# Sample attention over a paged cache: all keys before all values, keys turned by VectorE in 32x32 blocks, convolution taps by thirds

## The chip, the cores and the metric

The kernel runs on one core of one Trainium2 chip. The metric is the device time in microseconds (us) of one execution, as a median of repeated runs.

## The reference, cut to what matters

The kernel is one inference step of a two-layer decoder. A prompt (1024 tokens) and eight samples (4 tokens each) go through the same weights. The change touches layer 0, where one input projection feeds a gated convolution of width 3 and an attention with 4 heads; each head has two softmaxes whose difference weighs the values. For the samples, 2048 past keys and values of each lie in pages of 128 tokens, found through a page table:

```python
past_k = cache_k[j, page_table].reshape(nb, -1, DA_HEADS, 2 * DA_DIM)   # 8 samples, 16 pages each
keys = jnp.concatenate([past_k, k_rows], axis=1)      # 2048 past tokens and 4 own
s = jnp.einsum('bqhcd,bkhcd->bhcqk', q, keys) * (DA_DIM ** -0.5)
p = jax.nn.softmax(jnp.where(mask, s, -jnp.inf), axis=-1)
w = p[:, :, 0] - lam * p[:, :, 1]
attn = rmsnorm(jnp.einsum('bhqk,bkhe->bqhe', w, vals), subln_g) * (1.0 - lam_init)
y = ext[:, 0:s] * conv_w[0]                           # convolution: ext = [2 old rows, gate_c * xin]
for j in range(1, 3):
    y = y + ext[:, j:j + s] * conv_w[j]
y_conv = gate_b * y
mixed = jnp.concatenate([y_conv, attn], axis=-1) @ w_out
```

A feed-forward part, a second layer of another kind and its feed-forward part follow.

## The kernel before, in words

Activations lie transposed (features on the 128 partitions, 1056 tokens along the row), in three groups of 352 tokens. A projection is cut into *visits* (one block of 1024x128 weights, 512 KB, loaded by `load_tile`, split into two f16 parts by ScalarE in `split_hi` and VectorE in `split_lo`), and a visit into three *units*, one for each group: 24 f16 matmuls (L372), which `pe_halves` issues in two halves of 12. A unit's PSUM bank is drained by ScalarE or VectorE. In the stretch of this case visits 15 to 23 run, 27 units or 54 halves: for each of three groups of 128 convolution channels the gate `gate_c` (drained by ScalarE), `xin` (VectorE multiplies it into `conv_in`) and `gate_b` (VectorE multiplies it with the convolution's result, L1593). All 27 units use PSUM bank 7 alone.

Every engine's program is written out in order. `woven` takes one piece of the attention, then as many half units as a list of numbers says (`SAMPLE_FILL`), on every engine by the same list, so each engine passes the same places in the same order and waits on semaphores there.

The samples' attention (`pe_samples`, `act_samples`, `dve_samples`) runs in two rounds `r_` of four samples. A round has 32 steps for keys: two pages (a page is 128 tokens x 512 numbers of four bytes, 256 KB) are transposed by TensorE into PSUM (L1943), copied to `kt` by ScalarE (L2012) and VectorE (L2072), and scored one step later by four matmuls, one for each head, each in 32 columns of the array (L1931). Then maxima (L2067), exponentials (L2018) and weights (L1962, L1967), between which eight halves of units stand. Then 32 steps for values: two pages each, straight from the ring (L1982). The ring `ring` has 16 pages; `load_page` puts page f into slot f % 16 when `page_used` says that page f-16 is done with. SP and GpSimd issue these loads in turns of two; SP also issues the weight loads of the stretch. The stretch ends with the output projection (mix_ready, the first L372 over `arena`).

`pool_queries` lays out the samples' queries in `q_blk`; `tap` does one of the three convolution taps over all tokens, for a channel group's first unit of `gate_b`.

Of the kernel before, what the change touches and what calls it, by code (L numbers as in the profile page):

```python
# [18 lines left out]
ALU = mybir.AluOpType  # L19
# [59 lines left out]
def build(nc, x_p, x_s, cache_k, cache_v, state_conv, state_C, state_n, state_m, page_table, norms, w_in0,  # L79
# [3 lines left out]
    with ctx:  # L83
# [1359 lines left out]
        sm_max, sm_neg = small[:, 80:85], small[:, 85:86]  # L1443
        sm_sum, sm_scale = small[:, 86:91], small[:, 91:92]
# [4 lines left out]
        q_blk = arena[:, 19, 0:SEQ].rearrange("p (h b n) -> p h b n", h=HEADS, b=NB)  # L1449
        probs = flat2(20)[:, 0:2 * SEQ + TS]  # L1450
        wt = arena[:, 22, 0:SEQ].rearrange("p (k n) -> p k n", k=NPG)
        wt_own = arena[0:TS, 23, 0:64]
        comb = arena[:, 23, 64:128]
        kt = [arena[:, 24 + i, 0:SEQ].rearrange("p (h n) -> p h n", h=HEADS) for i in range(2)]
# [24 lines left out]
        kp_ev = [sem("kp_ev0"), sem("kp_ev1")]  # L1479
        kp_used = sem("kp_used")  # L1480
        own_t, max_ready, exps, comb_ready = sem("own_t"), sem("max_ready"), sem("exps"), sem("comb_ready")
        q_ready, o_zero = sem("q_ready"), sem("o_zero")
# [8 lines left out]
        def act_proj0(act, v0, v1_):  # L1491

            later = None
            for n in range(VISITS[v0].units[0], VISITS[v1_].units[-1] + 1):
# [9 lines left out]
                later = n if v >= CXB and m == 2 else None  # L1504
                yield
# [15 lines left out]
        def dve_proj0(dve, chain, v0, v1_):  # L1521
# [11 lines left out]
            def tap(h, k):  # L1533
                w = gains[:, GC + k * HC + h:GC + k * HC + h + 1]
                yp, ys = conv_y[:, 0:SEQ], conv_y[:, SEQ:T].rearrange("p (b t) -> p b t", b=NB)
                xp, xs = conv_p_in[:, k:k + SEQ], conv_s_in[:, :, k:k + NS]
                if k == 0:
                    dve.tensor_scalar(yp, xp, w, None, ALU.mult)
                    chain.link(dve.tensor_scalar(ys, xs, w, None, ALU.mult))
                elif k == 1:  # L1540
                    dve.scalar_tensor_tensor(yp, xp, w, yp, ALU.mult, ALU.add)
                    chain.link(dve.scalar_tensor_tensor(ys, xs, w, ys, ALU.mult, ALU.add))
                else:
                    chain.mark(dve.scalar_tensor_tensor(yp, xp, w, yp, ALU.mult, ALU.add))
                    dve.scalar_tensor_tensor(ys, xs, w, ys, ALU.mult, ALU.add).then_inc(gate_c_used, 1)
            for n in range(VISITS[v0].units[0], VISITS[v1_].units[-1] + 1):
                v, g, x = UNITS[n].visit, UNITS[n].g, ps[:, UNITS[n].bank, :]
                h, m = (v - CXB) // 3 if v >= CXB else v // 3, v % 3
                if v >= CXB and m == 2 and g == 0:
                    if h == 0:  # L1550
                        dve.wait_ge(q_ready, 1)
# [4 lines left out]
                    tap(h, 0)  # L1556
# [27 lines left out]
                if v >= CXB and m == 2:  # L1584
                    if g == 0:
                        tap(h, 1)
                        tap(h, 2)
                        dve.wait_ge(gate_c_used, h + 1)
                        chain.sync()
                        dve.wait_ge(yb_hi, 3 * h)  # L1590
                        dve.wait_ge(mix_ready, 3 * h)
# [222 lines left out]

        def dve_head(dve, chain, h):
# [24 lines left out]
            for i in range(8):  # L1840
# [3 lines left out]
                if i >= 4:  # L1844
# [4 lines left out]
                    yield  # L1849
                if i < 7:  # L1850
                    for hh, ii in next_scores(h, i):
                        dve_mixed(dve, chain, hh, ii)
                yield

        def pool_queries(pool, chain):

            pool.wait_ge(v_ev, 3 * HEADS - 1)
            drained(pool, last_unit(3 * HEADS - 3))
            chain.link(pool.memset(arena[:, 19, 0:SEQ], 0.0))
            for b in range(NB):  # L1860
                for c in range(2):
                    n = 8 * (b % 4) + 4 * c
                    ins = pool.tensor_copy(q_blk[64 * c:64 * c + 64, :, b, n:n + NS],
                                           qT[64 * c:64 * c + 64, :, SEQ + NS * b:SEQ + NS * b + NS])
            ins.then_inc(q_ready, 1)
# [15 lines left out]
        def sp_samples(sp):  # L1881
            f = RING
            for _ in range(3):
                yield
            for _ in range(2):
                for _ in range(32):
                    if f // 2 % 2 == 0 and f < 2 * NB * NPG:
                        load_page(sp, f)
                        load_page(sp, f + 1)
                    f += 2  # L1890
                    yield
                for _ in range(4):
                    yield
                for _ in range(32):
                    if f // 2 % 2 == 0 and f < 2 * NB * NPG:
                        load_page(sp, f)
                        load_page(sp, f + 1)
                    f += 2
                    yield
                for _ in range(3):  # L1900
                    yield

        def sp_proj0(sp, v0, v1_):
            for v in range(v0, v1_ + 1):
                load_tile(sp, v + 4)
                for _ in range(6):
                    yield

        def pe_samples(pe):
# [12 lines left out]
            pe.wait_ge(q_ready, 1)  # L1922
            for r_ in range(2):
                def scores(q):

                    n, b, j = 32 * r_ + q, 4 * r_ + q // 8, q % 8
                    pe.wait_ge(kp_ev[0], n + 1)
                    pe.wait_ge(kp_ev[1], n + 1)
# [1173 lines left out]
```

## Time and profile before

| | |
|---|---|
| median of 3 runs | 2687.76 us (2687.13 to 2693.2) |
| the profiled execution | 2693.54 us, its span 2691.9 us |
| mean granted TensorE clock | 0.992 of full speed |
| TensorE busy | 2623.9 us of the span |
| VectorE, ScalarE, GpSimd busy | 1242.1, 1026.6, 452.3 us |
| moved by DMA | 266.14 MB |

Engines in profile rows: PE is TensorE's matmul, PEld its weight load, DVE VectorE, ACT ScalarE, POOL GpSimd, SP SyncE. L1982 is a line of the kernel. A matmul of four-byte numbers shows as two records. A row of a group of instructions has the count behind an x; times are in us unless said.

### The profile page before, as it was taken

To read this page: it belongs to the slowest core of one execution; us is meant where nothing else is said; L and a number is where in the kernel's file an instruction comes from. 1 tells how busy PE (TensorE), PEld (TensorE's weight loads), DVE (VectorE), ACT (ScalarE), POOL (GpSimd) and SP (SyncE) were. 2 spreads that over 40 slices of the span, in tenths; PEclk is the share of its full clock that TensorE was granted. 3 is DMA by queue.
4 is the path that set the end of the run, shared out by engine and by line. 5 is a ranking of instruction groups with operands and counts; after the bars stand their busy time and mean duration, and the time that the engine had idled before them with its cause. 6 is when DMAs were issued, how large, how long until landed. Compare 5 with 4: busy or idle time off the path is not lost.

```text
span 2691.9 us, 49459 instructions
## 1 busy us (share of the span) xinstructions
PE 2623.9 (97%) x20217; PEld 1876.5 (70%) x20217; DVE 1242.1 (46%) x2042; ACT 1026.6 (38%) x1896; POOL 452.3 (17%) x529
## 2 busy tenths in 40 slices
PE   8999899999999999999999999999999999999998
PEld 5666566656688668886566766667657886788765
DVE  5555532326744214444754434344577441154454
ACT  4455322225444214433443333324365441244333
POOL 4001023222022002311101010110101220123121
PEclk9999999999999999999999999999999999999999
DMA  7211369761211312124434242322411122011442
GB/s 250 63 40 50 98 218 346 242 230 54 75 64 32 81 53 63 48 91 146 122 88 88 40 115 50 96 67 84 151 54 67 64 60 60 32 64 48 134 129 97
DMA packets 257659, 266.14 MB, mean 99 GB/s; under 512 B 10668, under 2 KB 217810, under 8 KB 256796
## 3 DMA queue, kind: packets, MB, share of 16 engines
q1 hardware_dynamic: 231772, 166.10, 22.0%
q0 software_dynamic: 25088, 94.79, 10.0%
q8 instruction: 162, 2.65, 0.4%
q10 hardware_dynamic: 576, 2.10, 0.2%
q14 instruction: 61, 0.50, 0.1%
HBM read 227.45 MB, written 35.50 MB: 98 GB/s over the span
## 4 chain that ended last, share of the span: by engine, by line
PE 90%; DVE 5%; ACT 2%; issue 1%; DMA 0%; POOL 0%; SPq 0%; DVEq 0%; ACTq 0%; POOLq 0%
PE ps L372 49%; PE ps L1130 25%; PE ps L1943 2%; PE ps L1931 1%; PE ps L1629 1%; PE ps L1982 1%; PE ps L1708 1%; PE ps L2477 1%; PE ps L2457 1%; PE ps L2491 1%; PE ps L2513 1%; DVE arena L883 1%; PE ps L1694 1%; PE ps L2500 1%; DVE hT L887 1%
## 5 line engine op out<-in xcount | busy, mean ns | idle before, releaser
L372 PE MATMUL ps<-u,w_split 128*128 128x352 f16 (+1 forms) x4752 | 752.3, 315 | 9.8 <-DVE u L737 5.9
L372 PEld LDWEIGHTS ps<-u,w_split 128*128 128x128 f16 (+1 forms) x4752 | 462.5, 98 | 260.3 <-issue 20.8
L372 PE MATMUL ps<-arena,w_split 128*128 128x352 f16 x3663 | 560.6, 313 | 3.7 <-DVE w_split L345 1.5
L372 PEld LDWEIGHTS ps<-arena,w_split 128*128 128x128 f16 x3663 | 357.6, 98 | 200.8 <-issue 9.5
L1130 PE MATMUL ps<-hT,w_split 128*128 128x264 f16 x3456 | 400.6, 276 | 3.2 <-ACT arena L1170 3.2
L1130 PEld LDWEIGHTS ps<-hT,w_split 128*128 128x128 f16 x3456 | 337.8, 98 | 54.8 <-DVE w_split L345 2.1
L345 DVE SCALAR_TENSOR_TENSOR w_split<-w_raw,w_split 128x1024 f16<-128x1024 f32 (+2 forms) x133 | 184.5, 1388 | 296.4 <-ACT w_split L329 295.8
L1130 PE MATMUL ps<-u,w_split 128*128 128x264 f16 x2592 | 303.4, 276 | 0.0
L1130 PEld LDWEIGHTS ps<-u,w_split 128*128 128x128 f16 x2592 | 253.6, 98 | 38.3
L329 ACT ACTIVATE w_split<-w_raw 128x1024 f16<-128x1024 f32 (+2 forms) x133 | 155.5, 1171 | 135.9 <-PE ps L372 97.3
L343 DVE SCALAR_TENSOR_TENSOR w_split<-arena,w_split 128x512 f16<-128x512 f32 x126 | 85.9, 723 | 103.9 <-ACT w_split L323 103.9
L1260 POOL TENSOR_TENSOR arena<-arena 128x512 f32<-128x512 f32 x18 | 22.8, 1265 | 527.2 <-DVE w_split L343 527.2
L343 DVE SCALAR_TENSOR_TENSOR w_split<-w_raw,w_split 128x512 f16<-128x512 f32 x126 | 80.8, 686 | 62.4 <-ACT w_split L323 62.4
L372 PE MATMUL ps<-arena 128*128 128x352 f16 x657 | 102.6, 316 | 0.0
L2327 ACT ACTIVATE arena<-ps 128x352 f32<-128x352 f32 x66 | 30.5, 464 | 179.7 <-PE ps L372 179.7
L817 POOL TENSOR_TENSOR arena<-arena 128x352 f32<-128x352 f32 x53 | 71.3, 1345 | 160.5 <-ACT arena L805 160.3
L1203 DVE TENSOR_TENSOR arena<-ps,arena 128x528 f32<-128x528 f32 x36 | 25.5, 707 | 153.1 <-ACT arena L1170 153.1
L1300 ACT ACTIVATE arena<-ps 128x352 f32<-128x352 f32 x48 | 22.3, 465 | 191.3 <-PE ps L372 191.3
L372 PEld LDWEIGHTS ps<-arena 128*128 128x128 f16 x657 | 64.5, 99 | 37.0 <-issue 3.1
L1216 DVE TENSOR_TENSOR arena<-arena 128x1056 f16<-128x1056 f32 (+1 forms) x60 | 58.3, 972 | 50.4 <-ACT arena L1153 41.4
L372 PE MATMUL ps<-u,arena 128*128 128x352 f16 x504 | 77.5, 313 | 3.2 <-ACT arena L1298 2.7
L323 ACT ACTIVATE w_split<-arena 128x512 f16<-128x512 f32 x126 | 71.7, 620 | 13.7 <-PE ps L1130 10.9
(405 smaller groups left out, 2989.4 us busy)
## 6 DMA issues: line engine op xcount, KB each, us to landing
w_raw<-in_w_down SPq DMA_DIRECT2D x58, 704.0 KB, 4.7
w_raw<-in_w_in SPq DMA_DIRECT2D x56, 512.0 KB, 7.9
arena<-in_w_gu SPq DMA_DIRECT2D x18, 1024.0 KB, 5.3
w_raw<-in_w_gu SPq DMA_DIRECT2D x18, 1024.0 KB, 5.2
hT<-in_cache_k SPq DMA_DIRECT2D x64, 256.0 KB, 4.4
hT<-in_cache_k POOLq DMA_DIRECT2D x64, 256.0 KB, 4.6
hT<-in_cache_v SPq DMA_DIRECT2D x64, 256.0 KB, 5.0
hT<-in_cache_v POOLq DMA_DIRECT2D x64, 256.0 KB, 5.5
```

The costliest lines, as they stand in the source:

```text
L323: act.activation(split_of(v, 0).rearrange("p (k n) -> p k n", k=kt), raw_of(v), ACT.Copy, scale=WS).then_inc(w_hi, 1)
L329: act.activation(split_of(v, 0)[:, 0:kt * n], raw_of(v), ACT.Copy, scale=WS).then_inc(w_hi, 1)
L343: dve.scalar_tensor_tensor(lo, raw_of(v), WS, hi, ALU.mult, ALU.subtract).then_inc(w_ready, 1)
L345: dve.scalar_tensor_tensor(split_of(v, 1)[:, 0:kt * n], raw_of(v), WS, split_of(v, 0)[:, 0:kt * n], ALU.mult, ALU.subtract).then_inc(w_rea ...
L372: ins = pe.matmul(ps[0:m, bank, 0:GW], split_of(v, wp)[:, k * w + col * P:k * w + col * P + m], x[:, xp, k0 + k, cols(g)], start=(k == 0 a ...
L817: pool.tensor_tensor(sum_y, sum_y, sq_y[k % 2], ALU.add).then_inc(y_added, 1)
L883: ins = dve.scalar_tensor_tensor(h_tmp[:, k % 2, :], ybuf[:, k, cols(g)], gains[:, col:col + 1], rs[0], ALU.mult, ALU.mult)
L887: dve.tensor_tensor(h, h, h_tmp, ALU.add).then_inc(h_ready, 1)
L1130: ins = pe.matmul(ps[:, bank + s_, 0:HW], split_of(v, wp)[:, k * P:(k + 1) * P], x, start=(name in ("M1", "M2", "M5") and k == 0 and q == ...
L1216: dve.tensor_tensor(hi_lo[:, 1], x, hi_lo[:, 0], ALU.subtract).then_inc(hid_ready, 1)
L1943: ins = pe.transpose(ps[:, 4 + e, h * P:(h + 1) * P], ring[:, f % RING, h * P:(h + 1) * P], ident[:, :])
L2327: act.activation((q_of[h % 2], k1, v1, o1)[m // 2][:, m % 2, cols(g)], ps[:, UNITS[n].bank, 0:GW], ACT.Sigmoid if m >= 6 else ACT.Copy, sc ...
```

## The change

All 128 pages of keys of the eight samples come first, then all 128 pages of values. A key page pair is turned by one VectorE instruction (`dve_turn`), which transposes each 32x32 block in place of the whole; so partition group i (32 partitions) holds, 32 features at a time, the tokens of group i, and a score is summed over four matmuls of 32 rows each, against query layouts that are rotated by 32 partitions (`q_turned`, made by DMA). Eight pages are scored together by 64 matmuls, in 4 row groups x 4 column groups, with row group i writing PSUM bank i. Turns run four steps ahead of the scores in VectorE's order. The two softmaxes stand among the key steps and the value steps, at step 32 and step 64. The weight loads of the stretch move from SP to ScalarE, the query copies ahead of the last head's stores on GpSimd, and the taps are done for a third of the tokens ahead of each unit of `gate_b`.

```diff
+        Q_ROWS = (10, 12, 13, 14)
+        q_turned = [arena[:, row, 0:SEQ].rearrange("p (h b n) -> p h b n", h=HEADS, b=NB) for row in Q_ROWS]
+        O_BANK = (6, 3)
+        turned = [rows(19 + 4 * i, 4)[:, :, 0:SEQ] for i in range(2)]
...
@@ act_proj0
+                if v >= CXB + 3 and g == 1:
+                    load_tile(act, v + 4)
@@ dve_proj0
-            def tap(h, k):
+            def tap(h, k, g):
...
+                a, b = g * GW, min(g * GW + GW, SEQ)
+                parts = [(conv_y[:, a:b], conv_p_in[:, k + a:k + b])]
...
-                    tap(h, 0)
+                if v >= CXB and m == 2:
+                    tap(h, 0, g)
...
+                    chain.sync()
+                    tap(h, 1, g)
+                    chain.sync()
+                    tap(h, 2, g)
+                    chain.sync()
...
+        def dve_turn(dve, q):
+            f = 2 * q
+            dve.wait_ge(page_loaded[f % RING // 2], 32 * (f // RING + 1))
+            if q >= 8:
+                dve.wait_ge(scored, q // 4 - 1)
+            dve.transpose(turned[q // 4 % 2][:, q % 4, :],
+                          ring[:, f % RING:f % RING + 2, :].rearrange("p r c -> p (r c)")).then_inc(page_used, 2)
@@ dve_head
+                if h == HEADS - 1 and i == 7:
+                    dve_turn(dve, 0)
@@ pool_queries
-            pool.wait_ge(v_ev, 3 * HEADS - 1)
+            pool.wait_ge(s_done, 16 * (HEADS - 1))
...
+            for s_ in range(1, 4):
+                cut = P - 32 * s_
+                pool.dma_start(arena[0:cut, Q_ROWS[s_], 0:SEQ], arena[32 * s_:P, Q_ROWS[0], 0:SEQ]).then_inc(q_ready, 16)
+                pool.dma_start(arena[cut:P, Q_ROWS[s_], 0:SEQ], arena[0:32 * s_, Q_ROWS[0], 0:SEQ]).then_inc(q_ready, 16)
-        ROUND_FILL = ((0,) * 32 + (2, 2, 2, 2) + (1, 0) * 15 + (0, 0) + (1, 1, 1))
-        SAMPLE_FILL = (1, 1, 0) + ROUND_FILL * 2
+        SAMPLE_FILL = ((1, 1, 0)
+                       + ((0, 0, 0, 1) + (0, 0, 0, 2)) * 3 + (0, 0, 0, 1) + (0, 0, 0, 4)
+                       + ((0, 0, 0, 1) + (0, 0, 0, 2)) * 4
+                       + (0, 0, 2, 0, 0, 0) * 10 + (0, 0, 2, 1)
+                       + (1, 1, 1))
@@ load_page
-            cache, b, p = (cache_k, cache_v)[f // 64 % 2], 4 * (f // 128) + f // NPG % 4, f % NPG
+            cache, b, p = (cache_k, cache_v)[f // (NB * NPG)], f // NPG % NB, f % NPG
@@ pe_samples
+            def scores(n):
+                b, j = n // 2, n % 2
+                pe.wait_ge(page_used, 8 * n + 8)
+                pe.wait_ge(exps, 9 * (n // 8))
+                pages = turned[j].rearrange("p a (e c) -> p a e c", e=2)
+                for s_ in range(4):
                     for h in range(HEADS):
+                        for i in range(4):
+                            part_, e0 = slice(32 * i, 32 * i + 32), P * h + 32 * ((i + s_) % 4)
+                            ins = pe.matmul(ps[32 * h:32 * h + 32, i, 256 * j:256 * j + 256],
+                                            q_turned[s_][part_, h, b, :], pages[part_, :, :, e0:e0 + 32],
+                                            start=(b % 4 == 0 and j == 0 and s_ == 0),
+                                            stop=(b % 4 == 3 and s_ == 3), skip_group_check=True)
+                ins.then_inc(scored, 1)
...
+            for q in range(64):
+                if q % 4 == 3:
+                    scores(q // 4)
+                if q % 32 == 31:
+                    own_scores(q // 32)
+                if q == 35:
+                    first_weights(0)
+                if q == 39:
+                    last_weights(0)
+                yield
+            for q in range(64):
+                values(q)
+                if q == 3:
+                    first_weights(1)
+                if q == 7:
+                    last_weights(1)
+                if q == 39:
+                    out_turned(0)
+                yield
@@ act_samples
+            def exponentials(r_):
                 act.wait_ge(max_ready, r_ + 1)
...
+                for i in range(4):
+                    for a in range(2):
+                        act.activation(probs[a].rearrange("p (f i t) -> p i f t", i=4, t=32)[:, i],
+                                       ps[:, i, 256 * a:256 * a + 256].rearrange("p (f t) -> p f t", t=32), ACT.Exp,
+                                       bias=sm_neg, accum_out=sm_sum[:, 2 * i + a:2 * i + a + 1]).then_inc(exps, 1)
...
+            for q in range(128):
+                if q in (32, 64):
+                    exponentials(q // 32 - 1)
...
@@ dve_samples
+            def maxima(r_):
                 dve.wait_ge(own_t, r_ + 1)
...
+            for q in range(128):
+                if q in (32, 64):
+                    maxima(q // 32 - 1)
+                if q in (33, 65):
+                    scales(q // 32 - 1)
+                if 5 <= q + 4 < 64:
+                    dve_turn(dve, q + 4)
...
@@ sync
-            woven(sp_samples(sp), sp_proj0(sp, CXB + 3, WO0 - 1), SAMPLE_FILL)
+            sp_samples(sp)
```

Turns 1 to 4 stand among the last head's tail in `dve_samples`, and turn 0 in `dve_head`.

## Rows read from the trace of the kernel before

**Rows 1.** The page: busy time, share of the span, instructions; the chain by engine.
```profile
PE 2623.9 (97%) x20217; PEld 1876.5 (70%) x20217; DVE 1242.1 (46%) x2042; ACT 1026.6 (38%) x1896; POOL 452.3 (17%) x529
...
PE 90%; DVE 5%; ACT 2%; issue 1%; DMA 0%; POOL 0%; SPq 0%; DVEq 0%; ACTq 0%; POOLq 0%
```

**Rows 2.** Busy us of PE, PEld, DVE, ACT, POOL by stage; clock, DMA share, GB/s.
```profile
318.00:367.00 49.00, 49.00 (x492) 31.11 (x491) 22.18 (x33) 18.53 (x31) 16.25 (x31) 0.99 0.93 314
368.00:391.00 23.00, 20.94 (x165) 14.72 (x162) 4.57 (x13) 6.70 (x15) 0.54 (x1) 0.93 0.21 71
402.00:437.00 35.00, 35.00 (x557) 21.76 (x558) 6.58 (x11) 4.78 (x8) 12.39 (x24) 1.00 1.04 374
447.00:495.00 48.00, 48.00 (x484) 30.58 (x482) 21.95 (x32) 18.04 (x31) 16.13 (x30) 1.00 0.95 322
```

**Rows 3.** TensorE in order of time, keys and first softmax: start, us, what [idle before].
```profile
315.25 3.67 PE L1943 MATMUL ps<-ident,hT 128*128 128x128 f32 x16 [1.86 <-issue]
...
330.01 0.64 PE L1931 MATMUL ps<-arena 128*32 128x256 f32 x8
330.58 1.09 PE L1943 MATMUL ps<-ident,hT 128*128 128x128 f32 x8
331.60 0.64 PE L1931 MATMUL ps<-arena 128*32 128x256 f32 x8
...
369.29 3.75 PE L372 MATMUL ps<-u,w_split 128*128 128x352 f16 x24
373.69 3.74 PE L372 MATMUL ps<-u,w_split 128*128 128x352 f16 x24 [0.65 <-ACT arena L1513]
378.84 0.30 PE L1960 MATMUL ps<-arena 128*32 128x64 f32 x2 [1.41 <-DVE arena L2086]
...
391.55 0.62 PE L1982 MATMUL ps<-hT,arena 128*4 128x128 f32 x16
```

**Rows 4.** TensorE in order of time, values and the end of the stage.
```profile
394.21 1.06 PE L1982 MATMUL ps<-hT,arena 128*4 128x128 f32 x32
395.20 1.96 PE L372 MATMUL ps<-u,w_split 128*128 128x352 f16 x12
397.10 1.06 PE L1982 MATMUL ps<-hT,arena 128*4 128x128 f32 x32
...
563.86 1.96 PE L372 MATMUL ps<-u,w_split 128*128 128x352 f16 x12
...
574.38 12.59 PE L372 MATMUL ps<-arena,w_split 128*128 128x352 f16 x72 [0.77 <-DVE arena L3016]
```

**Rows 5.** Waits, 300 to 575 us: us in total, times, longest.
```profile
POOL hT L1878 <- PE ps L1943: 134.3, 61, 64.0
```

**Rows 6.** Score matmuls (L1931) and weight loads under way, in slices of 0.03 us.
```profile
330.01:330.04 0.03, 0.03 (x4) 0.03 (x5) 1.00 0.53 205
330.04:330.07 0.03, 0.03 (x4) 0.03 (x8) 1.00 1.06 410
...
330.22:330.25 0.03, 0.03 (x5) 0.00 (x0) 1.00 0.89 342
```

**Rows 7.** TensorE in order of time, last head: row groups, and the tail's wait.
```profile
285.87 1.99 PE L1629 MATMUL ps<-arena 64*128 64x512 f32 x8
287.79 0.28 PE L1632 MATMUL ps<-causal,ident_b 128*128 128x128 bf16 x2
...
310.37 0.66 PE L1643 MATMUL ps<-ident,arena 128*128 128x128 f32 x4 [2.88 <-DVE arena L1806]
```

**Rows 8.** Groups of instructions, 312 to 574 us: busy us, mean ns of one.
```profile
L2067 DVE TENSOR_REDUCE small<-ps 128x1 f32<-128x512 f32 x8 | 5.5, 683 | 0.4 <-PE ps L1931 0.4
L2018 ACT ACTIVATE arena<-ps,small 128x512 f32<-128x512 f32 x8 | 5.4, 685 | 1.6 <-DVE small L2080 1.6
L1541 DVE SCALAR_TENSOR_TENSOR arena<-arena,gains 128x1024 f32<-128x1024 f32 x3 | 3.8, 1279 | 0.0
L1538 DVE TENSOR_SCALAR arena<-arena,gains 128x1024 f32<-128x1024 f32 x3 | 2.2, 748 | 0.0
```

More of the change, by code:

```diff
@@ L1881, in sp_samples @@
         def sp_samples(sp):
[L1882 to L1907, printed above, removed]
+            for f in range(RING, 2 * NB * NPG, 4):
+                load_page(sp, f)
+                load_page(sp, f + 1)
         def pe_samples(pe):
@@ L1921, in pe_samples @@
             pe.wait_ge(at_lo, 2 * HEADS)
[L1922 to L1928, printed above, removed]
-                    pe.wait_ge(exps, 5 * r_)
-                    for h in range(HEADS):
-                        ins = pe.matmul(ps[32 * h:32 * h + 32, j // 2, 256 * (j % 2):256 * (j % 2) + 256],
-                                        q_blk[:, h, b, :], kt[n % 2][:, h, :], start=(b % 4 == 0 and j % 2 == 0),
-                                        stop=(b % 4 == 3), skip_group_check=True)
-                    ins.then_inc(kp_used, 1)
-                if r_:
-                    pe.wait_ge(os_lo, 1)
-                for q in range(32):
-                    for e in range(2):
-                        f = 128 * r_ + 2 * q + e
-                        page_ready(f)
-                        pe.wait_ge(kp_ev[e], 32 * r_ + q)
-                        for h in range(HEADS):
-                            ins = pe.transpose(ps[:, 4 + e, h * P:(h + 1) * P], ring[:, f % RING, h * P:(h + 1) * P],
-                                               ident[:, :])
-                        ins.then_inc(page_used, 1)
-                    if q:
-                        scores(q - 1)
-                    yield
-                scores(31)
@@ L1993, in pe_samples, with values @@
-                yield
-                yield
+            def values(q):
+                r_, b = q // 32, q // 8 % 4
+                pe.wait_ge(wt_act, r_ + 1)
+                pe.wait_ge(wt_dve, 2 * r_ + 2)
+                pe.wait_ge(o_zero, r_ + 1)
+                for e in range(2):
+                    f, p = NB * NPG + 2 * q + e, (2 * q + e) % NPG
+                    page_ready(f)
+                    for h in range(HEADS):
+                        n = 16 * h + NS * b
+                        ins = pe.matmul(ps[32 * h:32 * h + NS, O_BANK[r_], b * P:(b + 1) * P],
+                                        wt_rows[r_][p // 4][:, p % 4, n:n + NS],
+                                        ring[:, f % RING, h * P:(h + 1) * P], start=(p == 0), stop=False,
+                                        skip_group_check=True)
+                    ins.then_inc(page_used, 1)
+                if q % 8 == 7:
+                    for h in range(HEADS):
+                        n = 16 * h + NS * b
+                        ins = pe.matmul(ps[32 * h:32 * h + NS, O_BANK[r_], b * P:(b + 1) * P], wt_own[r_][:, n:n + NS],
+                                        v_own[:, h, :], start=False, stop=True, skip_group_check=True)
+                    ins.then_inc(o_done, 1)
@@ L2849, in _ @@
             for h in range(HEADS):
+                if h == HEADS - 1:
+                    pool_queries(pool, chain)
                 for ev, src, dst, n in ((v_ev, v_nat, v_p, 2), (k_ev, k_nat, k_p, 2)):
```

217 lines of the change are left out of this document (106 added, 111 removed).

## The prediction

> **What bounds the kernel now.** I read the page first, for the engine that sets the end: TensorE is busy 97% of the span and makes 90% of the chain that ended last [rows 1]. So a change counts where it takes work off TensorE, or keeps it from waiting. Then the stretch that the diff rewrites, the samples' attention, from 315 us (first page turned) to 574.4 us (first output-projection matmul): busy times, clock and transfers by stage [rows 2]. TensorE has no idle time in a key round or a value round, VectorE and ScalarE are less than half busy there, and transfers run at 314 to 374 GB/s; in the softmax between keys and values they fall to 71 GB/s, and TensorE waits some. TensorE in order of time prices the key rounds [rows 3]: a set of scores starts at 330.01, the eight transposes of the next two pages at 330.58, the next scores at 331.60, so two key pages cost 1.59 us, of which 1.02 are transposes. 64 such rounds are 102 us. From 369.29, where the keys are scored, to 391.55, where values begin, pass 22.3 us, which hold four units of projection (8 halves of 1.9 us). The value part [rows 4] gives 0.50 us for two value pages, 1.9 us for half a unit, and 10.5 us from the last value to the end of the stage.
>
> In the waits GpSimd, which issues half of the page loads, waits 134 us in total for TensorE's transposes alone [rows 5]: the ring of 16 pages is full, and transfers follow TensorE. So what TensorE saves per page is worth its time only until transfers themselves can't follow; the best rate shown is 374 GB/s, 0.70 us for a page of 256 KB.
>
> **The change, part by part.** *Scores.* Gone: 512 transposes on TensorE, 64 VectorE copies and 64 ScalarE copies. New: 16 groups of 64 matmuls, each 32 rows, 32 columns of weights and 256 streamed columns, in sixteen tiles (four row groups, four column groups). What does a group cost? In the present scores four column tiles run together: four matmuls are in flight within 30 ns, and the second halves of the four join only 0.21 us later [rows 6]. So a set of four costs what one costs, about 0.43 us, and the start of another tile at most some 8 ns. That row groups run together too is seen in the heads [rows 7]: two row groups stream 1024 columns each, and the next line starts 1.92 us later; at the values' rate (0.22 us for 128 columns) one alone takes 1.74 us, and both in turn 3.5. Sixteen tiles at once give 4 x 0.43 plus start and end, 2.1 us for 8 pages. The bounds: below 1.9; above, four tiles at a time, 16 x 0.45 = 7.2 us (a rival). In between, if each record holds the issue for 27 ns (0.22 us for 8 records), 128 x 27 = 3.45 us. I take 2.1, since starts 8 ns apart are shown. Before, the same 8 pages cost 6.4 us.
>
> *Turns.* VectorE gets 64 block transposes of 128x1024 numbers of four bytes. None is in the trace. The nearest rows [rows 8]: 0.75 us for a one-operand multiply of 128x1024, 1.28 for one with two operands; a second pass over the data would make it 2.5. I take 1.2, with 0.75 and 2.5 kept for the range. With 1.1 us of its other work per unit (6.58 us in 35 us, six units [rows 2]) and the taps, VectorE needs 1.45 us per turn of two pages while keys run; transfers need 1.40, or 1.49 with the weights (nine blocks of 512 KB in the stage, 1.4 us each). So in the key stage TensorE (2 x 2.1 + 3 x 1.9 = 9.9 us for two groups) no longer sets the pace; turns and transfers do, 11.9 us.
>
> Only a page prices the turn itself: the Trainium skill, "Vector Engine (DVE) Microarchitecture Reference", section 3.8, says that the transposing front end sustains one element per cycle and lane; no run here shows it yet, and with the 0.96 GHz of "VectorE: DVE Perf Modes" (Specifications) 1024 elements would be 1.07 us, an estimate, by which the sum would be 3 to 4 us better.
>
> *Taps by thirds* are the same elements in nine pieces in place of six: some 0.3 us more VectorE per visit, hidden under VectorE's waits for units; without that cover nine units would pay 0.1 us each. *Weight loads from ScalarE*: each waits for VectorE's split two visits earlier, behind it stand ScalarE's drains of the gate units; that split comes three units before, so I price it at nothing; late, it would hold the single bank 7 and with it the next unit. On SP nothing but pages is left until the last page, so they no longer stand behind a weight load. *Query copies*: four layouts by 6 small DMAs on GpSimd's queue, in front of the stores of the last head. They need the scores of head 2 only, and GpSimd stands idle there. Nothing.
>
> Now the sum, by the clock of the trace of before.
> 1. Start. Turns 1 to 4 (4.8 us) stand among the last head's tail, where TensorE waits for VectorE already (2.88 us [rows 7]). I place half of them on the path: first scores at 317.4, not 315.25.
> 2. First half of the keys. VectorE is through turn 4 at 318.4, 27 more at 1.49 us end at 358.6; scores 2.1 and own scores 1.2 give 362. Ten half units are inside.
> 3. First softmax. TensorE has four halves to do (7.5, and 0.7 us for the drain of bank 7, as 0.65 in [rows 3]), to 370.2. But VectorE's maxima stand *behind* the drains of these same two units, not in front as now: 0.7 drain, 2.7 for four banks, 0.4 for the rest; then eight exponentials of 256 columns, between half and all of 0.69 us each [rows 8], 4.0 us taken. Scores of the next group wait for them: 378.0. That leaves a hole of 7.8 us in TensorE, where 1.41 us [rows 3] stands now.
> 4. Second half of the keys. VectorE has turns in store (the ring filled during the hole), so TensorE sets the pace: 8 x 2.1 + 10 x 1.9 + 4.4 weights + 1.2 own + four drains of 0.7 = 44.2, to 422.2. VectorE needs 28 x 1.2 + 8 = 41.6.
> 5. Values. The ring is full. In the next 15 us the second softmax lets only 24 value pages be loaded, 104 are left at 437.2: 104 x 0.70 + 4 weight blocks x 1.4 = 78.4, to 515.6, and 2.9 for what TensorE does behind the last pages: 518.5. TensorE by itself would be there at 507 (18.4 to the weights, 56 x 0.50, 20 x 1.9). Transfers win.
> 6. End. 10.5 as now and one more half, 12.4: 530.9 in place of 574.4.
>
> 43.5 us less. After 574.4 nothing is touched. The profiled execution took 2693.5 us (its span 2691.9 and 1.6 around it), 5.8 over the median of 2687.76; I take the saving off the median: 2644.
>
> For step 5 the Trainium skill has another rate: "DMA: Bandwidth & Descriptors", section "Where 436 GB/s comes from", puts what one core gets from HBM at about 358 GB/s. By that the 104 pages take 3.4 us longer. The trace goes above it (374 GB/s over 35 us [rows 2]), and the measurement decides.
>
> **The rivals.** *Four tiles at a time* (slower). If tiles of other row groups in the same columns must wait, or weight loads of the same row group do, a group costs 7.2 us. The loss against my sum is 16 x S - 38.4 us (in the first half S is hidden up to 2.7), which eats the gain at S = 5.2; at 7.2 it is 77, so 33 us slower: 2721. For it: no row shows both kinds of tiling at once. Against it: each is shown alone. 0.06. The Trainium skill speaks for it: "TensorE: Matmul & The Clock Gate", Part 3, says that a weight load overlaps matmuls in flight only when its row group differs, and here four loads with the same rows follow each other. By that rule a group would take 16 x 0.57 = 9.1 us and the kernel 2751; the trace does not agree, since in [rows 6] eight loads over all rows are there while matmuls of the first tiles run.
>
> *The turn takes two passes* (slower). At 2.4 us VectorE becomes the bound of the key stage: 27 x 2.4 + 5 to step 2, 30 us late, 31 more in step 4: 2705. It decides from 2.1 us. For it: four-byte numbers; against it: the other four-byte rows. 0.10.
>
> *Issue-bound scores*, S = 3.45: 17 us less gain, 2661. 0.10.
>
> *Transfers keep to 322 GB/s*, the rate of the second key round [rows 2]: 6 us in step 2, 12 in step 5: 2662. For it: most of the stage ran at that rate; against it: there the ring was what held them. 0.08.
>
> *Engines in step*: with bank 7 the only one for units, a unit's drain by VectorE stands behind four turns, 4.8 us. I count that as hidden, since TensorE waits for those turns anyway; if it isn't, seven such places cost 34 us: 2678. 0.10.
>
> **Numbers.** My forecast has 0.56: 2644, by itself from 2630 (transfers as fast as TensorE in step 5, 12 us) to 2658. A difference under 0.3% (8 us) is about what a measurement can't tell from none. Faster: 0.56 + 0.10 + 0.08 + half of engines in step 0.05 = 0.79; same 0.06 (the other half, and a little); slower 0.15 (0.06 + 0.10, less a little for a mild form). The range 2626 to 2682 holds the forecast and the three faster rivals, and leaves out those at 2705 and above.
>
> **What would show it.** A group of 64 scores at 2 us (4 or more: the rivals); the block transpose at 1.2 us; a TensorE hole near 370 us of some 7 us; transfers above 360 GB/s through the values, with TensorE waiting for pages there. Wrong would make me: turns over 2 us, tiles in turn, or drains that hold bank 7 through the key stage.

## The result and the profile after

The median is 2674.2 us (2667.91 to 2679.49, 7 runs) against 2687.93 for the kernel before on the same chip: ratio 0.9946, 95% interval 0.9932 to 0.9959. The interval lies below 1, so the kernel is faster, by 0.5%. The time is inside the range, but the gain is 13.7 us and not the 43.5 that the prediction worked out.

The group of the turns on the profile page of the changed kernel (busy us, mean ns of one):

```profile
L1832 DVE STREAM_TRANSPOSE arena<-hT 128x1024 f32<-128x1024 f32 x64 | 74.6, 1215 | 9.1 <-PE ps L1938 4.5
```

TensorE by stage, in answer to [rows 2] (us, PE busy, granted clock, DMA share, GB/s): first key half, second key half.

```profile
314.00:362.00 48.00, 42.37 (x1155) 1.00 0.98 341
378.00:436.00 58.00, 50.73 (x1194) 0.92 0.79 270
```

TensorE in order of time, in answer to [rows 3, 4]: stops in the first key half, then from the first own scores to the start of the values.

```profile
332.42 2.63 PE L1938 MATMUL ps<-arena 32*32 32x256 f32 x114 [1.14 <-issue]
...
338.44 1.67 PE L372 MATMUL ps<-u,w_split 128*128 128x352 f16 x10 [1.20 <-issue]
...
344.45 0.65 PE L1938 MATMUL ps<-arena 32*32 32x256 f32 x11 [1.76 <-issue]
...
361.78 0.90 PE L1950 MATMUL ps<-arena 128*32 128x32 f32 x32
362.61 3.75 PE L372 MATMUL ps<-u,w_split 128*128 128x352 f16 x24
367.56 3.74 PE L372 MATMUL ps<-u,w_split 128*128 128x352 f16 x24 [1.19 <-DVE arena L1605]
378.62 4.75 PE L1938 MATMUL ps<-arena 32*32 32x256 f32 x128 [7.32 <-ACT small L2035]
...
407.70 2.76 PE L1938 MATMUL ps<-arena 32*32 32x256 f32 x128
410.39 0.32 PE L372 MATMUL ps<-u,w_split 128*128 128x352 f16 x1
414.01 2.66 PE L372 MATMUL ps<-u,w_split 128*128 128x352 f16 x11 [3.30 <-issue]
416.60 3.35 PE L1938 MATMUL ps<-arena 32*32 32x256 f32 x116
420.30 0.65 PE L1938 MATMUL ps<-arena 32*32 32x256 f32 x12 [0.35 <-issue]
...
425.38 3.37 PE L1938 MATMUL ps<-arena 32*32 32x256 f32 x128
...
430.57 1.98 PE L1938 MATMUL ps<-arena 32*32 32x256 f32 x79
434.06 1.36 PE L1938 MATMUL ps<-arena 32*32 32x256 f32 x49 [1.51 <-issue]
...
436.52 3.75 PE L372 MATMUL ps<-u,w_split 128*128 128x352 f16 x24
440.21 1.49 PE L1979 MATMUL ps<-hT,arena 128*4 128x128 f32 x48
441.63 3.75 PE L372 MATMUL ps<-u,w_split 128*128 128x352 f16 x24
445.31 0.62 PE L1979 MATMUL ps<-hT,arena 128*4 128x128 f32 x16
448.31 0.30 PE L1957 MATMUL ps<-small 128*32 128x64 f32 x2 [2.37 <-DVE small L2116]
```

Three things are to be seen. The hole of 7.3 us ahead of 378.62 is there as forecast, and behind that idle time the group runs 4.75 us: the granted clock is 0.50 from 378 to 384 us, the lower of its two levels, 1.2 GHz. A group of scores (next start less own start) takes 2.69 us, not 2.1. And three times in each key half TensorE stops in the middle of a group or unit with no releaser ("issue"). The stop at 434.06 is in the last group of the second half, after 79 of its 128 records.

The start of the value stage in windows of 4 us, TensorE's waits for pages in it (us in total, times, longest), and its end in order of time:

```profile
436.00:440.00 4.00, 4.00 (x53) 1.00 0.00 0
440.00:444.00 4.00, 4.00 (x66) 1.00 0.47 96
444.00:448.00 4.00, 1.94 (x26) 1.00 0.87 318
448.00:452.00 4.00, 3.69 (x26) 0.62 0.33 119
452.00:456.00 4.00, 4.00 (x73) 0.53 0.50 143
```

```profile
PE ps L1979 <- DMA hT<-in_cache_v: 12.4, 10, 3.7
```

```profile
544.83 3.75 PE L372 MATMUL ps<-u,w_split 128*128 128x352 f16 x24
551.17 3.52 PE L372 MATMUL ps<-u,w_split 128*128 128x352 f16 x12 [2.59 <-DVE arena L1605]
...
559.92 0.60 PE L3123 MATMUL ps<-ident,conv_new 128*18 128x128 f32 x4 [2.90 <-DVE arena L1536]
561.30 3.94 PE L372 MATMUL ps<-arena,w_split 128*128 128x352 f16 x14 [0.77 <-DVE arena L3078]
```

In the first 8 us of the value stage almost nothing is transferred. Behind the wait of 2.37 us for the second softmax (at 448.31) the clock is 0.62 and 0.53 from 448 to 456 us, and the transfers are slow again. The stage ends at 561.30, against 574.38 [rows 4] before and 530.9 forecast: 30.4 us later than forecast. Set against the prediction's steps: the second half's first scores 0.6 late (378.62 for 378.0); step 4, from there to the end of the second own scores (436.52), 57.9 for 44.2, 13.7 more; step 5, to the last value (544.83), 108.3 for 96.3, 12.0 more; step 6 16.5 for 12.4, 4.1 more. From the stage's end to the end of the span it is 2113.9 us, 2117.5 before; in the experiments it lies between 2111 and 2118 whatever was edited, and no cause is sought in it. All readings in order of time are of one profiled execution for each kernel (2676.81 us for the changed one).

### The profile page after: what moved, and what is told of

It reads as the page before. It is cut to its first block, busy times and chain, and to the rows that moved or that the text cites. A ratio compares the mean times of both kernels' runs of the same rounds, so it can differ in the third digit from the quotient of the medians.

```text
span 2675.2 us, 51317 instructions
## 1 busy us (share of the span) xinstructions
PE 2572.8 (96%) x21241; PEld 1843.9 (69%) x21241; DVE 1273.7 (48%) x2063; ACT 987.5 (37%) x1848; POOL 454.7 (17%) x535
## 4 chain that ended last, share of the span: by engine, by line
PE 73%; DVE 4%; ACT 2%; issue 1%; POOL 0%; DVEq 0%; ACTq 0%
PE ps L372 40%; PE ps L1130 25%; PE ps L2538 1%; PE ps L2518 1%; PE ps L2552 1%; PE ps L2574 1%; DVE arena L883 1%; PE ps L2561 1%; DVE hT L887 1%; DVE arena L897 1%; PE ps L2602 1%; PE ps L2553 1%; PE ps L786 0%; PE ps L991 0%; DVE w_split L345 0%
## 5 line engine op out<-in xcount | busy, mean ns | idle before, releaser
L1300 ACT ACTIVATE arena<-ps 128x352 f32<-128x352 f32 x48 | 22.2, 463 | 191.4 <-PE ps L372 191.4
L1832 DVE STREAM_TRANSPOSE arena<-hT 128x1024 f32<-128x1024 f32 x64 | 74.6, 1215 | 9.1 <-PE ps L1938 4.5
```

The lines of the kernel that those rows point to most:

```text
L1832: dve.transpose(turned[q // 4 % 2][:, q % 4, :], ring[:, f % RING:f % RING + 2, :].rearrange("p r c -> p (r c)")).then_inc(page_used, 2)
```

## Experiments

The theory after the result: in the second key half TensorE is held by the longer score group and by late instructions, in the value stage by a late start of the transfers and by page waits after which the clock falls. Rivals: the scores' own length explains all of step 4; the transfers' rate explains step 5. All kernels but e2 are edits of the changed kernel.

**e1_maxima_first**: the softmax ahead of the units' drains.

```
 VectorE:  q in (32, 64): maxima -> q in (31, 63);  q in (33, 65): scales -> q in (32, 64)
 ScalarE:  q in (32, 64): exponentials -> q in (31, 63)
```

> The changed kernel with the maxima and exponentials of both softmaxes ahead of the units that follow the last scores of the round, not behind their drains. If the hole of 7.3 us ahead of the ninth score group is made by that order, and TensorE's half clock in the group behind it (4.7 us in place of 2.7) by the hole, both go: the own scores of the second round end 8 to 10 us earlier, at 427 us, and the 2.4 us wait before the second weights too; the kernel is 7 to 11 us faster than the changed one, 2663 to 2667 us. Rival: the turns and the page loads set the pace of the second key half, since VectorE turns nothing during the softmax; then the hole only moves into the key groups behind it, and the gain is under 3 us.

Measured: 2668.54 us, ratio to before 0.9917 (0.9904 to 0.9930). ScalarE, VectorE and TensorE in order of time:

```profile
369.29 1.10 ACT L329 ACTIVATE w_split<-w_raw 128x1024 f16<-128x1024 f32 x1
```

```profile
370.42 1.23 DVE L345 SCALAR_TENSOR_TENSOR w_split<-w_raw,w_split 128x1024 f16<-128x1024 f32 x1 [4.58 <-ACT w_split L329]
```

```profile
373.47 5.50 PE L372 MATMUL ps<-u,w_split 128*128 128x352 f16 x24 [7.76 <-DVE arena L1605]
378.89 2.76 PE L1938 MATMUL ps<-arena 32*32 32x256 f32 x128
```

The hole did not close, it moved: a weight split now stands behind the exponentials on ScalarE, VectorE waits for it with the drain (L1605) behind, and the second unit, which needs the same bank 7, waits for that drain. What was gained lies behind: the wait ahead of the second group's weights (2.37 us at 448.31) is gone, and the values end 100.5 us after the second own scores (433.58) instead of 108.3. Yet the stage opens in the same order and as empty of transfers; what differs comes later, with the clock at 1.00:

```profile
436.00:440.00 4.00, 4.00 (x66) 1.00 0.22 37
...
448.00:452.00 4.00, 4.00 (x43) 1.00 0.92 282
452.00:456.00 4.00, 3.67 (x90) 1.00 1.00 346
```

**e2_taps_only**: the kernel before, with the taps by thirds and nothing else.

```
-def tap(h, k):  whole row, all three thirds at g == 0
+def tap(h, k, g):  one third at each g
```

> The kernel before with nothing but the taps by thirds. In the changed kernel the last head's tail stands 2.8 us earlier than before, ahead of anything of the samples. If that is the taps (three times 1056 elements no longer stand in one piece ahead of the first drain of a gate unit), this kernel is about 3 us faster there and some 0.5 us for each of the three channel groups in the samples' stage: 2683 to 2685 us against 2688. Rival: the 2.8 us come from the query copies and the turn in the head; then it is within 1 us of the kernel before.

Measured: 2688.36 us, ratio 0.9996 (0.9987 to 1.0005). TensorE, the last head and the stage's end:

```profile
307.90 0.66 PE L1649 MATMUL ps<-ident,arena 128*128 128x128 f32 x4 [2.88 <-DVE arena L1812]
...
574.19 6.03 PE L372 MATMUL ps<-arena,w_split 128*128 128x352 f16 x28 [0.77 <-DVE arena L3022]
```

The last head's tail comes 2.5 us earlier than in [rows 7], and the stage ends where it did. The taps alone are worth nothing that can be measured.

**e4_quarter_pages**: only one head of each page (64 KB of 256) is loaded, the rest of the ring keeps old numbers, so scores and values are of wrong data; all instructions stay.

```
-ring[:, f % RING, :], cache[0, ds(page, 1), :, :, :]
+ring[:, f % RING, 0:P], cache[0, ds(page, 1), :, 0:1, :]
```

> The changed kernel with a quarter of each page loaded (the columns of one head; the rest of the ring keeps old numbers, so the outputs of the samples are others). Every instruction of the engines stays. If TensorE's stops in the middle of a score group or of a unit (1.1 to 3.3 us, six of them between 330 and 435 us, with no releaser) are late instruction fetches behind saturated page transfers, they go; if the value stage is held by transfers and by the clock that falls in its waits, it takes TensorE's own 88 to 92 us from the own scores to the last value, not 108. Then the stage ends 25 to 32 us earlier, kernel near 2645. Rival: the stops belong to the stream of small matmuls itself and stay; then only the value stage shrinks and the second key half keeps 58 us.

**e7_half_scores**: leaves out half of the score products (two of four row-group shifts).

```
-for s_ in range(4):
+for s_ in (0, 3):
```

> The changed kernel with two of the four score matmuls of each tile (half of the sum over features is left out, so the outputs of the samples are others). TensorE's instructions in a group fall from 256 with the weight loads to 128. If the scores' own time counts only where TensorE sets the pace, the first key half keeps its length within 2 us (turns and transfers set it), and the second loses 8 times 1.3 us and its stops: own scores of the second round at 420 to 424 us in place of 436.5, kernel 12 us faster than the changed one. Rival: turns set the pace in both halves, then it gains under 4 us.

**e9_half_columns**: all products, each over half of the pages.

```
-ps[32 * h:32 * h + 32, i, 256 * j:256 * j + 256], ... pages[part_, :, :, e0:e0 + 32]
+ps[32 * h:32 * h + 32, i, 256 * j:256 * j + 128], ... pages[part_, 0:2, :, e0:e0 + 32]
```

> Leaves out the scores of half of the pages: each of the 64 products of a score group streams 128 columns instead of 256; the number of instructions is unchanged. If a group is paced by the streamed columns, it takes about 1.4 us like the group with half of the instructions (1.42), and the stops ahead of score groups with no releaser shrink only with the shorter work. If it is paced by the issue of its 128 products and 128 weight loads, it stays at 2.5 to 2.7 us. If the stops come from the fetch of instructions, they remain (some 5 us in the second key half), since just as many instructions are fetched, in less time.

Measured, one run each: e4 2641.62, e7 2652.65, e9 2690.31 us. TensorE's waits with no releaser from 312 to 440 us (us in total, times, longest), in the changed kernel:

```profile
PE ps L1938 <- issue: 7.2, 5, 2.5
PE ps L372 <- issue: 4.5, 2, 3.3
```

in e4, in e7 and in e9:

```profile
PE ps L1938 <- issue: 2.0, 1, 2.0
```

```profile
PE ps L1938 <- issue: 2.5, 1, 2.5
```

```profile
PE ps L1938 <- issue: 16.9, 10, 2.6
PE ps L372 <- issue: 5.3, 2, 4.4
```

The wait of 2 to 2.5 us that all four have is that of the first group, ahead of which the tail ends. The others go when the transfers are a quarter (same instructions) and go when the instructions of the scores are half (full pages); in e7 TensorE waits 8.7 us for turns as well, which leaves instructions time to come. In e9, where the same instructions stand for less work, the waits nearly double: 22.2 us for 11.7. In e9 the second own scores start at 440.29, later than with all columns (435.36), at a clock of 0.84 from 384 to 440. So TensorE here needs instructions faster than they come while pages fill the DMA engines. The instruction queue (q8) fits: in the changed kernel a packet starts in the half microsecond behind 410.9 (queue: packets, MB, share of 16 engines) and takes 1.1 us (13.7% of 16 x 0.5), within the stop that ends at 414.01.

```profile
q8 instruction: 1, 0.02, 13.7%
```

So do the others. Packets of this queue start at 329.76, 336.00, 342.10, 411.38, 417.95 and 431.71 us; each of the six stops ends 1.2 to 1.6 us behind the end of one of these transfers. In e9 all eleven stops behind the first group's do the same (1.2 to 1.5 us).

e4 gives the other shares of step 4: with no stops and a clock of 0.94 the second key half takes 49.1 us, so the longer group and its slow start behind the hole are worth about 5 of the 13.7. A group takes 2.69 us in e4 too, 1.42 with half of the products (and so of the columns), 1.84 with half of the columns alone: fewer columns do not shorten it in proportion, fewer products do. The value stage of e4 takes 88.2 us, with 2.0 us of waits for pages, though the wait for the second softmax (2.4 us) is there.

**e10_heads_inner**: the order of the products.

```
-for h in range(HEADS):
-    for i in range(4):
+for i in range(4):
+    for h in range(HEADS):
```

> The same products in another order: the loop over the four heads (column groups of the array) is inside, the loop over the four row groups outside, so that successive products share their row group. By the rule of the Trainium skill, TensorE: Matmul & The Clock Gate, Part 3, that a weight load is hidden only under a product of another row group, a score group should grow from 2.69 us to 4 or more, the key halves by over 10 us each. If the array takes the sixteen tiles in any order, the group stays at 2.6 to 2.8 us and the time at 2674 within 2.

Measured: 2683.44 us, one run; TensorE in order of time:

```profile
405.46 2.75 PE L1938 MATMUL ps<-arena 32*32 32x256 f32 x128
```

The group is the same, 2.69 us from start to start. The Trainium skill, "TensorE: Matmul & The Clock Gate", Part 3, says that a weight load overlaps products in flight only when its row group differs. By that rule the order should matter; in this kernel's trace it does not. The run is 9 us longer: its stops are elsewhere (12.7 us in all for 11.7; last own scores at 441.03), and the clock is 0.93 in the first key half, where the changed kernel has 1.00. One run does not say more.

**e5_single_halves**: units in the value stage one half at a time.

```
-(0, 0, 2, 0, 0, 0) * 10
+(0, 0, 1) * 20
```

> In the value stage the fill is a half unit after every third pair of pages' step in place of a whole unit after every sixth; the amount of work is the same. If the 16 pages of the ring fill up while TensorE is in a whole unit (3.75 us, 5.6 at the half clock) and it then stands at a page and loses the clock, the time from the end of the second own scores to the end of the values falls from 108 us by 4 to 10, the waits for pages from 12.4 us to under 6, and the median from about 2674 to 2664 to 2670. If the stage is held by the transfers alone, both stay: 108 us and 2674 within 2.

Measured: 2678.05 us, ratio 0.9954 (0.9938 to 0.9971), page waits 13.1 us for 12.4, values 112 us behind the own scores. Missed: whole units between the values are not what holds the stage. What stayed is its start: the first weights still wait, 4.17 us for the softmax, and the clock is 0.84 in the 15 us behind the own scores.

**e11_values_first**: the values open the stage.

```
-(0, 0, 2, 0, 0, 0) * 10 + (0, 0, 2, 1)
+(0,) * 8 + (0, 0, 2, 0, 0) * 11 + (1,)
-TensorE, values: first_weights(1) at q == 3, last_weights(1) at 7
+TensorE, values: first_weights(1) at q == 11, last_weights(1) at 15;  their copies 8 steps later
```

> The value stage begins with eight pairs of value pages in a row; the second group's first weights come after the twelfth pair instead of the fourth, its last weights after the sixteenth instead of the eighth, and the projection units lie behind the first eight pairs, two halves after every third of each five pairs. The work is the same. In the changed kernel the transfers move 0, 96, 318 and 119 GB/s in the four stretches of 4 us from 436, because TensorE opens the stage with a unit and later waits for the second softmax while the ring is full. If that lost start is what step 5 of the prediction left out, the 8 us come back: from the end of the second own scores to the end of the values 98 to 101 us instead of 108, median 2663 to 2667. If the stage is held by the transfers' rate or the clock all through, it stays at 106 to 110 and 2674 within 2.

Measured: 2668.85 us (2661.72 to 2677.12), ratio 0.9924 (0.9894 to 0.9954). Windows, and TensorE in order of time:

```profile
440.00:444.00 4.00, 2.75 (x100) 1.00 0.72 235
...
448.00:452.00 4.00, 4.00 (x42) 1.00 1.03 388
```

```profile
434.24 0.90 PE L1950 MATMUL ps<-arena 128*32 128x32 f32 x32
...
528.55 0.40 PE L1987 MATMUL ps<-arena,small 32*4 32x128 f32 x8
```

From the second own scores to the last value 94 us instead of 108.3 (98 to 101 expected). No weights wait for the softmax; from 450 to 526 us the clock is 1.00 and the transfers run at 368 GB/s, where the changed kernel has 0.88 and 326 GB/s from 451.5 to 540.5. So the transfers can run faster here than in the changed kernel. But the edit opens the transfers earlier and takes away the wait for the softmax, and other kernels part the two: e1 and e12 keep the opening and lose the wait, and take 100.5 and 100.2 us (e8, with half a unit less in front, 99.3). Most of the loss of step 5 is thus the wait and what follows it; what the earlier transfers are worth (here 94 for about 100) is not settled, since e13 below has them too and takes 103. As a time e11 can't be told from the changed kernel: the intervals overlap, and the profiled execution (2664.72) lies below the median.

**e8_unit_earlier**: e1 with one unit moved from the second key half into the first.

```
-((0, 0, 0, 1) + (0, 0, 0, 2)) * 3 + ...        ; ((0, 0, 0, 1) + (0, 0, 0, 2)) * 4
+(0, 0, 0, 2) * 2 + ((0, 0, 0, 1) + (0, 0, 0, 2)) * 2 + (0, 0, 0, 2) + ... ; (...) * 2 + (0, 0, 0, 1) * 4
```

> As e1_maxima_first, with one projection unit moved from the second key half into the first, so that the weight split which stood behind the exponentials on ScalarE in e1 falls into an earlier unit. In e1 the second fill unit waited 7.76 us for a drain that stood behind that split. If this wait is what kept e1 from closing the hole, the second group half of scores starts at about 372.5 instead of 378.9, and the second key half is shorter by one unit (3.9 us): own scores end near 426 against 433.6, median about 2661 to 2664. If the hole is only the softmax's own length (maxima, exponentials, scales), the start stays near 378 and the median within 2 of e1's 2668.5.

Measured: 2670.2 us, ratio 0.9919 (0.9902 to 0.9936). Missed:

```profile
377.75 5.96 PE L372 MATMUL ps<-u,w_split 128*128 128x352 f16 x24 [8.81 <-DVE arena L1605]
```

The split was out of the way, but the same drain stood behind the low part of the unit before (L1536), which waits for ScalarE's high part (L1506), and that stood behind the exponentials.

**e12_hole_closed**: own scores, half a unit, then the softmax; two turns behind the maxima. **e13_both**: with e11. **e14_one_unit**: e13 with one unit in the hole.

```
 all three engines: one more step at q == 31, behind the own scores; there maxima, exponentials; scales at q == 32
 VectorE: turns 34 and 35 behind the maxima
-fill there (0, 0, 0, 4)
+fill there (0, 0, 0, 1, 3)      e14: (0, 0, 0, 1, 1), the other unit at the end of the values
```

> The maxima stand behind the own scores and half a unit, ahead of two of the next turns and of the drain; the exponentials stand right behind the weight split and the high part of that half unit, the scales ahead of the next turns. All units of this stage use one bank, so the second unit in the hole needs the first one's drain: in e1 and e8 that drain stood, by way of the split or the high part, behind the exponentials. If that order makes the hole, the second half's first scores start 9 to 11 us after the first own scores' end instead of 16, at about 372 to 373.5, the half clock there goes, and the median is 2664 to 2668. If the hole is the length of maxima plus exponentials plus scales themselves, the start stays at 378 and the time at e1's 2668.5 or above.

> The edits of e12_hole_closed and e11_values_first together. If the two lie in different stretches, as the stage reading has it, their gains add: 2655 to 2661. If the earlier end of the keys only meets the same transfers sooner, the sum is that of the better one, about 2664 to 2667.

> e13_both with one projection unit in the hole behind the first own scores instead of two; the other unit goes into the value stage, where TensorE stood 14 us at pages in e13. In e12 the second unit of the hole waited 4.19 us for the first one's drain, which stood behind two turns, the weight split and the taps, and then ran 6.3 us at the half clock. If that unit, not the softmax, holds the scores, the second half's scores start 7 to 8 us after the first own scores' end (14.2 in e12, 16.0 in the changed kernel), the keys end 6 to 7 us earlier and, with the unit hidden under page waits, the median is 2657 to 2662. If the value stage has no room for the unit or the clock falls in the shorter hole as well, it stays at e13's 2666 within 2.

Measured: e12 2663.88 us, ratio 0.9897 (0.9881 to 0.9914); e13 2666.44, 0.9904 (0.9887 to 0.9921); e14 2661.55 (2659.25 to 2673.85), 0.9896 (0.9879 to 0.9913). In e12 the scores come 14.2 us behind the own scores (9 to 11 expected, 16.0 in the changed kernel), still behind the second unit. TensorE in e14, and in e13 at the start of the values:

```profile
366.43 3.75 PE L372 MATMUL ps<-u,w_split 128*128 128x352 f16 x24
373.32 4.21 PE L1938 MATMUL ps<-arena 32*32 32x256 f32 x128 [3.14 <-ACT small L2037]
```

```profile
442.73 2.31 PE L1979 MATMUL ps<-hT,arena 128*4 128x128 f32 x32 [3.60 <-DMA hT<-in_cache_v]
446.43 1.03 PE L1979 MATMUL ps<-hT,arena 128*4 128x128 f32 x16 [1.40 <-DMA hT<-in_cache_v]
447.40 5.98 PE L372 MATMUL ps<-u,w_split 128*128 128x352 f16 x24
```

With one unit the scores start 6.9 us behind the own scores (7 to 8 expected), the softmax itself, and the keys end at 428.24 instead of 436.52. But the two gains do not add: in e13 TensorE is through the ring's pages before new ones land, stands 3.60 and 1.40 us, and then runs a unit in 5.98 us where 3.75 is usual (clock 0.50 from 444 to 452); from the own scores to the last value e13 and e14 take 103 us, 9 more than e11 (e14 with one unit more in the stage, and in an execution of 2669.85 us, 8 above its median). e12, e13 and e14 can't be told from each other; the intervals of all three lie below that of the changed kernel.

## Why the prediction was right in direction and wrong in size

**Steps 1 and 2 were right in their sum, by luck.** The first own scores end at 362.61 (362 forecast). But the first scores start at 314.18 and not at 317.4, and the half takes 48.4 us for 44.6. Step 2 had turns and transfers set the pace, "11.9 us" for two groups; in this half TensorE waits for no turn and no page. It set the pace itself, with groups of 2.69 us and three stops for instructions (1.14 + 1.20 + 1.76 = 4.1 us). With quarter pages (e4) the half takes 45.1 us, with half of the products (e7) TensorE does wait for turns.

**Step 3 and the turn were right.** The turn is 1.215 us (1.2 taken), the next scores start at 378.62 (378.0), with a hole of 7.3 us (7.8). e14 brings the 16 us between own scores and scores down to 6.9 with the maxima ahead and one unit, so the softmax behind the drains of two units made the rest. The Trainium skill's price of the turn ("Vector Engine (DVE) Microarchitecture Reference", section 3.8, with the clock of "VectorE: DVE Perf Modes", Specifications) gave 1.07 us as an estimate; measured is 1.215.

**Step 4 failed: "TensorE sets the pace: 8 x 2.1 + ... = 44.2".** It took 57.9. The term 2.1 measured 2.69, 4.7 us in eight groups. Two things were left out of the sum. Stops for instructions: 3.30 + 0.35 + 1.51 = 5.2 us. And the lower clock behind waits and stops: the group at 378.62 takes 4.75 for 2.76, those at 416.60 and 425.38 (3.37) some 0.6 to 0.9 each too long, the unit at 414.01 (11 of its 12 records in 2.66, where 12 take 1.95) another 0.9: about 4.5 with the weights. Less 1.4 for the drains, which cost 0.81 and 0.64 in place of 2.8, this is 13.0 of 13.7. *Issue-bound scores* (3.45) is nearest among the rivals, but not what it was: the supply of instructions held TensorE, and only while pages filled the transfers.

**Step 5 failed: "104 x 0.70 + 4 weight blocks x 1.4 = 78.4".** Its start came as forecast: 142 GB/s over the 15 us behind 436.5 are 8 pages, and with the 16 in the ring the 24 of the sum. The last page landed at 540.4, so the other 104 took 88.9 us with three weight blocks among them, 0.81 us a page instead of 0.70; TensorE's end behind them took 4.4 for 2.9. The sum had transfers at full rate from there on ("Transfers win") and left out the clock. Behind the wait of 2.37 us for the second softmax, TensorE took 3.32 us for weights and 3.60 for four pairs of pages, 2.00 and 1.93 in e1. From 448 to 456 it freed few pages (119 and 143 GB/s); then it stood at pages, 12.4 us in ten waits, with the clock at 0.90 from 455 to 545. The three kernels without that wait are 8 to 9 us shorter in this stage, e5 with a wait of 4.17 us is 4 longer, and e5 excludes the size of the units. e4 has the wait and quarter pages and takes 88.2, so the wait costs this much only where full pages can't catch up. The empty first 8 us are not the main loss: e1 and e12 have them too. The mean of 320 GB/s from 455 to 545 was no limit: 368 GB/s are seen over 76 us (e11) and 386 over 20 us (e5, 475 to 495), so the rival *transfers at 322* had the number and not the reason. The Trainium skill's "DMA: Bandwidth & Descriptors", section "Where 436 GB/s comes from", puts what one core gets from HBM at about 358 GB/s; these measurements go above it.

**Step 6**: 16.5 us for 12.4. Behind a wait of 2.59 us for a drain the next half unit runs slowly (3.52 for 1.95), and the transposes of the convolution's new rows (L3123) wait 2.90 for the low part, where before it was 1.77 (the taps' last third stands ahead of it; e2 shows the same 2.90).

**The rivals that fell**: four tiles at a time (2.69 us for a group of sixteen tiles, in either order of loops), two passes in the turn. For the first, the prediction read four loads with the same rows in a row; in this kernel the row group changes with each product, and it is e10 that has that order. *Engines in step* by bank 7 was not the cost in the key stage (waits of 0.6 to 0.8 us), but it is what kept the hole open in e1, e8 and e12.

**What stays open.** Where the late instruction packets waited is not in the trace: it shows their transfer (0.9 to 1.4 us each, with full and with quarter pages), not when they were asked for. That transfers make them late rests on e4, e7 and e9 together. Why a group takes 2.69 us and not 2.1 is not shown; half of the columns alone leave 1.84 of it. How the loss of step 5 divides between the wait, the clock behind it and the later page waits is argued from the order of time; no run changes one of them alone. That e13 and e14 lose the clock at the start of the values and e11 does not is seen, and no run tells how to avoid it with the keys ended earlier.

## What to carry to other kernels

Where a sum makes transfers the bound of a stage, follow the engine that frees their buffers too, with its waits and its clock: here a wait of 2.37 us was followed by 8 us at a clock of 0.62 and 0.53, in which the transfers fell to 119 and 143 GB/s, and the stage lost far more than the wait. A step whose end comes out right can hold two errors that cancel; look at the waits before calling it right. Many small products save TensorE's columns but not its instructions; count both, and look for stops with no releaser while transfers are full. A softmax moved ahead of other work helps only as far as nothing that the work needs stands behind it on any of the engines.

## What had not been expected of the hardware

Stops of 0.35 to 3.3 us with no releaser in the middle of a group of products or a unit, each ending 1.2 to 1.6 us behind the transfer of an instruction packet, gone when the pages were a quarter. Halving the columns of 1024 products left the kernel 16 us slower than the changed one (2690.31, one run). Sixteen tiles of 32 rows and 32 columns run 64 fp32 products of 256 columns in 2.69 us, the same in both orders of the loops. VectorE's block transpose of 128x1024 numbers of four bytes took 1.215 us.
